# Three of the four weight sums of a seven-product matrix multiplication made by VectorE instead of by accumulating transfers, with X parked in memory

## The reference, cut to what matters

```
h = rmsnorm(x, g[2])
f = square(relu(h @ mlp_w1)) @ mlp_w2     # 2048 -> 8192 -> 2048
x = x + rmsnorm(f, g[3])
```

## Time and profile before

| what | value |
|---|---|
| median of 3 runs | 2440.25 us |
| profiled execution | 2433.57 us, span 2431.7 us |
| mean granted TensorE clock | 0.978 |
| busy: TensorE matmul, weight load | 2312.5 us, 1898.8 us |
| busy: VectorE, ScalarE, GpSimd | 1623.3, 1321.8, 127.4 us |
| read from memory | 559.77 MB |

### The profile page before, as it was taken

The page is one execution under the profiler, slowest core; times in us unless marked ns, Lnnn a source line. Parts: engine busy times, 40 slices in busy tenths (PEclk is TensorE's granted clock), DMA queues, the critical chain, the costliest instruction groups (busy, mean ns, idle before and its releaser), DMA issues.

```text
span 2431.7 us, 26613 instructions
## 1 busy us (share of the span) xinstructions
PE 2312.5 (95%) x10609; PEld 1898.8 (78%) x10609; DVE 1623.3 (67%) x2015; ACT 1321.8 (54%) x1769; POOL 127.4 (5%) x160
## 2 busy tenths in 40 slices
PE   9999999999889899899999989899899899999998
PEld 6778888778778677777887777787777788888887
DVE  5665856866667667667877667667666676556764
ACT  6355445655646556555666646556556555444453
POOL 0000000001001001010001000000000001000000
PEclk9999999999999999999999999999999999999999
DMA  8444545889899898896658898998998845653343
GB/s 332 157 173 173 184 164 190 239 279 275 277 278 254 262 294 254 257 283 228 225 208 233 272 289 252 262 293 264 254 283 269 251 141 201 244 214 129 140 172 121
DMA packets 80299, 563.60 MB, mean 232 GB/s; under 512 B 9033, under 2 KB 9364, under 8 KB 14319
## 3 DMA queue, kind: packets, MB, share of 16 engines
q1 hardware_dynamic: 61568, 429.58, 47.1%
q0 software_dynamic: 18464, 132.20, 26.2%
q10 hardware_dynamic: 144, 0.12, 0.0%
HBM read 559.77 MB, written 2.10 MB: 231 GB/s over the span
## 4 chain that ended last, share of the span: by engine, by line
PE 59%; DMA 23%; DVE 9%; ACT 4%; issue 2%; POOL 1%; ACTq 0%; POOLq 0%; DVEq 0%
PE P L351 56%; DMA R_f<-in_w_u 15%; DVE low L614 7%; DMA raw<-in_w_d 5%; ACT hi L495 3%; DMA raw<-in_w_u 3%; PE P L354 3%; DVE EV L599 1%; DVE R_m L599 1%; ACT EV L551 1%; POOL raw L1002 0%; ACT R_h L490 0%; POOL R_f L1007 0%; DVE R_f_r L599 0%; DVE X L602 0%
## 5 line engine op out<-in xcount | busy, mean ns | idle before, releaser
L614 DVE TENSOR_TENSOR low<-raw,hi 128x1024 fp32r<-128x1024 f32 (+3 forms) x752 | 879.6, 1203 | 535.8 <-ACT hi L495 532.7
L495 ACT ACTIVATE hi<-raw 128x1024 fp32r<-128x1024 f32 (+3 forms) x752 | 758.3, 1039 | 551.2 <-PE P L351 315.4
L351 PE MATMUL P<-hi,R_h 128*128 128x512 f32 (+2 forms) x2944 | 954.9, 395 | 8.4 <-DVE low L614 8.1
L351 PE MATMUL P<-hi,R_f_r 128*128 128x512 f32 x2480 | 822.4, 405 | 96.7 <-DVE R_m L599 52.7
L351 PEld LDWEIGHTS P<-hi,R_h 128*128 128x128 f32 x2944 | 554.4, 189 | 131.4 <-DVE low L614 12.7
L351 PEld LDWEIGHTS P<-hi,R_f_r 128*128 128x128 f32 x2480 | 483.7, 195 | 211.9 <-DVE low L614 109.1
L351 PE MATMUL P<-low,R_h 128*128 128x512 f32 (+2 forms) x1472 | 572.4, 389 | 0.0
L351 PE MATMUL P<-low,R_f_r 128*128 128x512 f32 x1240 | 497.6, 401 | 0.0
L614 DVE TENSOR_TENSOR low<-R_f,hi 128x1024 fp32r<-128x1024 f32 x224 | 264.5, 1221 | 94.1 <-ACT hi L495 92.4
L351 PEld LDWEIGHTS P<-low,R_h 128*128 128x128 f32 x1472 | 278.0, 189 | 56.3 <-issue 4.3
L495 ACT ACTIVATE hi<-R_f 128x1024 fp32r<-128x1024 f32 x224 | 227.7, 1052 | 100.6 <-DMA R_f<-in_w_u 66.4
(11 more groups left out here) (216 smaller groups left out, 1260.4 us busy)
## 6 DMA issues: line engine op xcount, KB each, us to landing
raw<-in_w_d SPq DMA_DIRECT2D x128, 1024.0 KB, 8.4
raw<-in_w_u SPq DMA_DIRECT2D x100, 1024.0 KB, 5.2
R_f<-in_w_u POOLq DMA_DIRECT2D x84, 1024.0 KB, 11.9
raw<-in_w_z SPq DMA_DIRECT2D x46, 1024.0 KB, 4.9
raw<-in_w_i SPq DMA_DIRECT2D x36, 1024.0 KB, 4.8
R_f<-in_w_u SPq DMA_DIRECT2D x28, 1024.0 KB, 7.9
raw<-in_w_u POOLq DMA_DIRECT2D x28, 1024.0 KB, 10.4
raw<-in_w_mo SPq DMA_DIRECT2D x16, 1024.0 KB, 4.9
```

The source lines that it names most:

```text
L351: return self.e.matmul(o, l, r, start=start, stop=stop, skip_group_check=True)
L495: self.e.activation(hi, raw, ACT.Copy).then_inc(*self.inc("high_made", ("high", k, d)))
L614: self.e.tensor_tensor(low, raw, hi.bitcast(f32), ALU.subtract).then_inc(*self.inc("low_made", *lows))
```

## The change

T1, T2 and T3 are made by VectorE. A new `tile_sum` adds two tiles that lie on chip, one 128x2048 instruction each, six in a round. b12 needs two more buffers: these are the two rows of X (`chain[2]`, `chain[3]`), so GpSimd writes X to a memory tensor `x_kept` before the rounds and reads it back after them. b22 is loaded once a round into the ring for product 3, and is kept there until T2 and T3 have been made from it. T4 alone is still an accumulating transfer. Product 2 adds on to product 1 in the same bank (a copy of product 1 is taken first), and product 3 on to product 5; with this two additions of VectorE a round go. Besides: the fourth tile of the kernel lands in `R_f` at once instead of waiting for the ring; and where an MLP or layer begins, two pieces of work of the stage before are issued ahead of two quarter splits.

```diff
+FIRST = 3
-        self.chain = [R_f[:, 4096:6144], R_f[:, 6144:8192]]
+        self.chain = [R_f[:, 4096:6144], R_f[:, 6144:8192], self.X[:, 0, :], self.X[:, 1, :]]
+        self.first_raw = R_f[:, 0:2048]
+    def tile_sum(self, o, i, ready, done):
+        self.wait_ge(ready)
+        self.tt(o, o, i, ALU.add, done)
...
     def link(mlp_, e, s, j, free):
+        w = a[f"w_u{mlp_}"]
+        if s in (0, 1):
+            return
+        if s == 2:
+            E.chain_add(j, m.chain[j], w[8 * e + CHAIN[s + 1] + j], free, ("chained", mlp_, e, s + 1, j))
+        elif e == 7:
+            chain_last[j + 2 * (s == 4)] = free
+        elif s == 3:
+            E.chain_load(j, m.chain[j], w[8 * e + 8 + j], free, ("chained", mlp_, e + 1, 0, j))
         else:
+            E.chain_load(j + 2, m.chain[j + 2], w[8 * e + 12 + j], free, ("linked", mlp_, e + 1, j))
...
             quarter = quarters()
+            out_of(0)
+            squares_of(0)
             quarter(0)
             quarter(1)
-            out_of(0)
-            squares_of(0)
...
+        def keep_x():
+            kept = side_load("kept", a["x_kept"], m.X.rearrange("p t n -> p (t n)"), list(x_m))
+            for j in range(2):
+                E.chain_load(j + 2, m.chain[j + 2], a[up_w][12 + j], [kept, list(h_m), list(r_m)], ("linked", l, 1, j))
...
                 for k in range(4):
-                    x = ready[4 * n + k] if isinstance(ready, list) else ready
+                    x = [ready[4 * n + k] if isinstance(ready, list) else ready, onto]
...
             def third(b, done):
-                k = ev(hold=True)
-                ks[12] = k
-                ms[12] = combine(k, P[b][:, :], EV[ks[5]][:, :], ALU.add, [done, ms[5]], ev_free[k])
-                bank_free[b] = [ms[12]]
+                box["w"] = b, done
             def sixth(b, done):
                 ms[1] = combine(ks[1], P[b][:, :], EV[ks[1]][:, :], ALU.add, [done, ms[1]])
                 bank_free[b] = [ms[1]]
-                c12 = combine(ks[12], EV[ks[12]][:, :], EV[ks[1]][:, :], ALU.subtract, [ms[12], ms[1]])
-                ms[12] = relu_square(ks[12], EV[ks[12]][:, :], 0, c12, None)[1]
-                ms[1] = c12
+                wb, w_done = box["w"]
+                ks[12] = k = ev(hold=True)
+                c12 = combine(k, P[wb][:, :], EV[ks[1]][:, :], ALU.subtract, [w_done, ms[1]], ev_free[k])
+                bank_free[wb] = [c12]
+                ms[12] = relu_square(k, EV[k][:, :], 0, c12, None)[1]
...
+            def first_sum(j):
+                E.tile_sum(m.chain[j], m.chain[j + 2], [("chained", l, e, 0, j), ("linked", l, e, j)], ("chained", l, e, 1, j))
+            def second_sum(j):
+                k = kept_at + j
+                landed = None if listing else plan[k][6]
+                E.tile_sum(m.chain[j], m.raw[(landed or 0) % NL][:, :], [("chained", l, e, 1, j), ("loaded", k)], ("chained", l, e, 2, j))
+            def third_sum(j):
...
+                E.tile_sum(m.chain[j + 2], m.raw[(landed or 0) % NL][:, :], [("linked", l, e, j), ("loaded", k)], done)
...
-            down(0)
-            up(2, 1, HH[:, HRIGHT, TOP], HL[:, HRIGHT, TOP], h_right, plain(b21), second)
+            down(0, lambda: first_sum(0))
+            up(2, 0, HH[:, HRIGHT, TOP], HL[:, HRIGHT, TOP], h_right, plain(b21), second, onto=ms[1], aside=(lambda: first_sum(1), nop))
...
-            up(5, 0, SH[1], SL[1], s_m[1], linked(1), fifth)
-            down(2)
-            up(3, 1, SH[4], SL[4], s_m[4], plain(b22), third)
+            up(5, 1, SH[1], SL[1], s_m[1], linked(1), fifth)
+            down(2, lambda: third_sum(0))
+            up(3, 1, SH[4], SL[4], s_m[4], plain(b22, "kept"), third, onto=ms[5], aside=(lambda: second_sum(0), lambda: second_sum(1)))
             down(3)
-            up(6, 0, SH[2], SL[2], s_m[2], linked(2), sixth)
+            up(6, 0, SH[2], SL[2], s_m[2], linked(2), sixth, aside=(lambda: third_sum(1), nop))
             down(4)
-            up(7, 1, SH[3], SL[3], s_m[3], added, seventh)
+            up(7, 1, SH[3], SL[3], s_m[3], linked(4), seventh)
...
+        back = [side_load(f"back{t}", m.X[:, t, :], a["x_kept"][:, 2048 * t:2048 * t + 2048], chain_last[2 + t]) for t in range(2)]
```

More of the change, by code:

```diff
@@ L997, in side_load @@
         self.e.dma_start(o, i).then_inc(*self.landed(sem, done))
-    def add_tile(self, k, o, i, l):
-        self.wait_ge(("loaded", k))
-        self.e.dma_start(o, i, accum_op=ALU.add).then_inc(*self.landed(f"sum{l % NL}", ("tile sum", k)))
     def chain_add(self, j, o, i, free, done):
@@ L1010, with load_tile @@
 class Sync(Engine):
-    def load_tile(self, k, o, i, l, free):
+    def load_tile(self, k, o, i, ring, free):
         self.wait_ge(free)
-        self.e.dma_start(o, i).then_inc(*self.landed(f"ring{l % NL}", ("loaded", k)))
+        self.e.dma_start(o, i).then_inc(*self.landed(ring, ("loaded", k)))
     def chain_load(self, j, o, i, free, done):
@@ L1070, in load_ahead @@
                     return
[L1071 to L1074, removed]
+                E.load_tile(k, m.raw[l % NL][0:parts, 0:c], a[name][i], f"ring{l % NL}", freed.get(l - NL))
+            elif k == FIRST:
+                E.load_tile(k, m.first_raw, a[name][i], "ring3", None)
             at_["load"] += 1
@@ L1081, in split_part @@
         if kind == "chain":
-            raw, ready = m.chain[more[3]], ("chained", *more)
+            raw, ready = m.chain[more[3] + 2 * (more[2] == 4)], ("chained", *more)
+        elif k == FIRST:
+            raw, ready = m.first_raw, ("loaded", k)
         else:
-            raw, ready = m.raw[l % NL], ("tile sum", k) if kind == "sum" else ("loaded", k, 2 * d // n) if k < 2 else ("loaded", k)
+            raw, ready = m.raw[l % NL], ("loaded", k, 2 * d // n) if k < 2 else ("loaded", k)
         free = None
@@ L1092, in split_part @@
                 link(*more, ("low", k, 3))
-            else:
+            elif kind == "load" and l is not None:
                 freed[l] = ("low", k, 3)
@@ L1097, in link @@
     def link(mlp_, e, s, j, free):
[L1098 to L1103, removed]
-        else:
-            E.chain_add(j, m.chain[j], a[f"w_u{mlp_}"][i], free, done)
-    chain_last = [None, None]
+        w = a[f"w_u{mlp_}"]
[7 more added lines that the diff above has]
+            E.chain_load(j, m.chain[j], w[8 * e + 8 + j], free, ("chained", mlp_, e + 1, 0, j))
+        else:
+            E.chain_load(j + 2, m.chain[j + 2], w[8 * e + 12 + j], free, ("linked", mlp_, e + 1, j))
+    chain_last = [None] * 4
     def split_ahead(n):
@@ L1137, in take @@
             l = o = None
-            if kind != "chain":
+            if kind != "chain" and j != FIRST:
                 l = numbers["landing"]
@@ L1899, in both_ways, with copied @@
         def both_ways(e, up_banks, down_banks):
[L1900 to L1903, removed]
+            b21, b22 = ([8 * e + n + j for j in range(2)] for n in (2, 6))
+            plain = lambda b, kind="load": [(i, kind) for i in b]
+            linked = lambda s: [(8 * e + j, "chain", (l, e, s, j)) for j in range(2)]
             ks, ms, box = {}, {}, {}
+            def copied(n, b, done):
+                k, name = ev(hold=True), mark("product copied")
+                E.copy_out(EV[k][:, :], P[b][:, :], done, ev_free[k], name)
+                ks[n], ms[n] = k, name
             def first(b, done):
[L1907 to L1910, removed]
+                copied(1, b, done)
             def second(b, done):
-                k = ev(hold=True)
[L1914 to L1918, removed]
+                ks[11] = k = ev(hold=True)
+                evacuated, ms[11] = relu_square(k, P[b][:, :], 0, done, ev_free[k])
+                bank_free[b] = [evacuated]
             def fifth(b, done):
[L1921 to L1924, removed]
+                copied(5, b, done)
             def third(b, done):
-                k = ev(hold=True)
-                ks[12] = k
-                ms[12] = combine(k, P[b][:, :], EV[ks[5]][:, :], ALU.add, [done, ms[5]], ev_free[k])
-                bank_free[b] = [ms[12]]
+                box["w"] = b, done
             def sixth(b, done):
@@ L1949, in fourth, with up @@
                 ms[1] = relu_square(ks[1], EV[ks[1]][:, :], 1, c21, None)[1]
+            kept_at = at_["take"] + 9
+            def first_sum(j):
[4 more added lines that the diff above has]
+                E.tile_sum(m.chain[j], m.raw[(landed or 0) % NL][:, :], [("chained", l, e, 1, j), ("loaded", k)], ("chained", l, e, 2, j))
+                if not listing and j == 0:
+                    freed[landed] = ("chained", l, e, 2, j)
+                    load_ahead()
+            def third_sum(j):
+                k = kept_at + j
+                landed = None if listing else plan[k][6]
+                done = ("chained", l, e, 4, j)
+                E.tile_sum(m.chain[j + 2], m.raw[(landed or 0) % NL][:, :], [("linked", l, e, j), ("loaded", k)], done)
+                if not listing and j == 1:
```

(10 more changed lines are left out.)

12 lines of the change are left out of this document (7 added, 5 removed).

## The result

The changed kernel takes 2363.07 us (median of 4 runs, 2362.51 to 2364.74) against 2438.41 (median of 4, 2434.93 to 2447.19) beside it: 0.9687 of the time, 95% interval 0.966 to 0.9714, 75 us less. The forecast was 2396 us, with a range of 2340 to 2436. Its profiled execution took 2364.74 us, 1.7 above its median, where that of before lay under its own.

A forecast was written before the change was run, and what follows sets the result against it. MLP rounds were taken to wait for accumulating transfers. Full rounds -46, openings +6, start -3 and stage beginnings -1 made -44 us against the profiled 2433.57, so 2390; with 6.7 to the median, 2396 us, range 2340 to 2436.

The forecast's parts named there:

- What bounds the kernel: MLP rounds wait for accumulating transfers, one of 25.64 us; a full round loses 10.3 us against 83.6.
- Rival B: Full rounds: no difference, T4's transfer takes 25.6 us, not 11.9; round at 94, kernel 2440 us; chance 0.09.
- VectorE in a full round: VectorE's order makes TensorE wait 0.3 us at d4 and 3.7 at product 7, 4.0 in all, bounds 0 and 8.
- Rival A: Full rounds: everything hidden, no wait reaches the slow clock, rounds of 84 to 85 us, kernel 2322 us; chance 0.22.
- rival C: Full rounds: slower, VectorE sets the pace and all six sums hold up splits; round 99.3, kernel 2512 us; chance 0.09.
- The clock: Behind the wait at product 7, the slow clock costs 2.5 us a full round, between 0 and 3.4.
- PSUM banks: Holding banks instead of rotating: no price at products 1 and 2 or 5 and 3; at product 7 the 3.7 us wait.
- Opening rounds: Two opening rounds: first two sums cost 3.9 us in full; +3 us each, +6 together, bounds 0 and +12.
- X to memory and back: Write of X before the rounds and reading back after: 0; 4 us each if SyncE were needed.
- The start: Kernel's start: the fourth tile lands earlier, -3 us (0 to -4).
- The stage beginnings: Where a stage begins, two places: quarter splits leave the path, -1 us in all (0 to -2.6).
- From the profile to the median: Step from profiled execution to median of runs: the median lies 6.7 us above, taking 2390 to 2396.

The follow-up runs named there:

- e5: Kernel before the change, its eight accumulating transfers a round cut to an eighth of their width, the rest of the sums left out: 2290.8 us, ratio 0.9384.
- e8: Kernel before the change with only the change's use of the banks, all sums by accumulating transfers: 2436.19 us, ratio 0.9974.
- e10: On top of e2, ScalarE's relu and square behind products 6, 7 and 4 issued one d tile later: 2317.32 us, ratio 0.9494.
- e12: On top of e10 with product 3 copied out at once, the last two quarters of X loaded at the kernel's start: 2311.14 us, ratio 0.9477.
- e1: Changed kernel, but ScalarE copies product 3 out of bank 1 at once and c12 is made from the copy: 2338.45 us, ratio 0.9552.
- a1: The changed kernel itself, unaltered, run again beside other experiments: 2364.84 us, ratio 0.9697 to the kernel before.
- e4: Changed kernel with VectorE's six sums a round cut to half their width, the other half left out: 2293.81 us, ratio 0.9396.
- e7: Changed kernel with its side edits undone (fourth tile waits for the ring, quarter splits first again): 2370.2 us, ratio 0.972.
- e2: Changed kernel with the two additions behind product 6 put ahead of the split of T3's second tile on VectorE: 2337.18 us, ratio 0.9547.
- e3: Changed kernel with the edits of e1 and e2 together: 2341.27 us, ratio 0.9563.
- e6: Changed kernel with 12 further 128x512 matmuls ahead of product 7, written to a bank nobody reads: 2343.37 us, ratio 0.9571.

## Why the prediction was right, and where it was off

**What bounds the kernel.** Right: the MLP rounds wait for accumulating transfers (e5). Wrong in the name of the place: I called the product behind the late transfer product 6, and the tile d4. Product 6's pair of additions had run at 1533.35 already; the pair at 1548.20 is product 7's, the tile that waits is d6, and the transfer of 25.64 us is T4's. The first of product 6's two additions, and GpSimd's issues in time with what stood beside T4's transfer, in the kernel before:
```profile
1533.35 0.68 DVE L599 TENSOR_TENSOR EV<-P,EV 128x512 f32<-128x512 f32 x1
...
1514.49 0.86 POOL L1002 DMA_DIRECT2D raw<-in_w_u  x1 [17.23 <-DMA raw<-in_w_u]
1518.10 0.86 POOL L1002 DMA_DIRECT2D raw<-in_w_u  x1 [2.74 <-DMA raw<-in_w_u]
1518.63 2.11 POOL L1007 DMA_DIRECT2D R_f<-in_w_u  x2
```
T4's two additions stood behind T3's two. GpSimd's order cost them little: T2's splits, which they wait for, ended at 1515.1 and 1517.9, and they were issued at 1518.6 and 1519.2. Then four additions were under way at once and landed about 7 us apart, at 1523.2, 1530.0, 1537.4 and 1544.8. e8 has the same, 26.6 us. Rival B lived from that number; with T3's additions gone T4's land in 8.0 us, and B is out.

**VectorE in a full round.** Right in mechanism, place and nearly size: forecast 0.3 us at d4 and 3.7 at product 7, measured 0.4 and 3.0 of standing (0.6 and 3.1 by the gaps between matmuls); no other wait. The dense round: 83.6, measured 83.42 (e5). Rival A stopped at the order, as forecast, and with the order mended (e10 to e12) its rounds of 84 to 85 us are there; rival C would have needed waits elsewhere, and there were none.
**The clock** was the term sized too high: 2.5 us a round for 1.7 (3.4 us at the 1.2 GHz level in each of the twelve). A round came out at 88.87 for 90.1. The old one is 94.41 over the twelve rounds, not the 93.96 that eleven gave: the gain was 5.5 us a round, 66 us, for 46.
**PSUM banks** (the Trainium skill, Perfetto Trace Analysis, Matmuls, on rotating banks): no price at product 2 and 3, as said. At product 7 a half of the answer: TensorE did wait at the bank, yet with the bank free (e1) 2.9 us of the 3.3 stayed. What the bank cost was one long wait in place of short ones, which is to say the clock.
**Opening rounds**: +6 forecast, -0.8 measured, and +0.8 in the second trace of the changed kernel (a1). The failed step is the 3.9 us for the two first sums: d2, the first tile behind VectorE's long stretch, starts 29.2 us into the round before and 31.3 to 31.5 after, so they cost 2.2. They went in part into time in which VectorE had stood for ScalarE, in the kernel before:
```profile
482.81 1.22 DVE L599 TENSOR_TENSOR R_h<-R_m,R_h 128x1024 fp32r<-128x1024 f32 x1 [2.40 <-ACT R_h L490]
```
The wait at product 7, 3.3 us by the gaps, came as forecast, the clock behind it not always. Busy time by stretch behind it, first and second opening round of the changed kernel:
```profile
519.20:522.60 3.40, 3.40 (x15) 2.84 (x16) 1.13 (x1) 3.37 (x5) 0.00 (x0) 1.00 1.00 424
1309.60:1316.20 6.60, 5.75 (x14) 4.52 (x15) 4.19 (x4) 4.45 (x6) 0.00 (x0) 0.50 1.00 423
```
No slow clock in one, twice the usual in the other: this is most of what parts their 91.5 and 94.2 us. In a1 the first had 3.4 us of it and took 93.0. With the sums halved (e4) both take 85.6.
**X to memory and back**: 0 forecast; the part of the trace that holds the write is 0.1 us shorter. Right.
**The start**: wrong. -3 forecast, +0.8 measured here, and -1.0 on the mean of thirteen traces (e7 above). The wait for the fourth tile went, 1.9 us; a longer one came behind it, for a split that stands on ScalarE behind the squares of X's last rows, whose load was queued behind three weight tiles. TensorE's waits near 36 us in the changed kernel, and ScalarE in time:
```profile
PE P L353 <- DVE low L616: 3.4, 1, 3.4
```
```profile
33.84 0.63 ACT L523 ACTIVATE EV<-X 128x512 f32<-128x512 f32 x1 [5.70 <-DMA X<-in_x]
...
36.40 1.99 ACT L497 ACTIVATE hi<-raw 128x1024 fp32r<-128x1024 f32 x2
```
e12 shows it: rows earlier, 4.7 us less. The same start differs by 0.9 us in two executions of the changed kernel (320.2 and 321.1), so a microsecond there is not to be told apart in one pair.
**The stage beginnings**: -1 forecast, -2.4 measured; at the last one (3.4 us of wait before, 1.75 after) the slow clock went as well, though in e2's trace it stood behind a wait of the same length.
**From the profile to the median**: I added 6.7 us, the old execution's place below its median. The new one lay 1.7 above. With the 44 us forecast of the profile against 68.8, this is the rest of the 33 us by which the forecast was too high. The parts did not cancel each other: full rounds 20 us, openings 7, stage beginnings 1 and this step 8 all went one way, the start 4 the other.

## What to carry to other kernels

Lay a tight stretch out in the order of its busiest engine, tile by tile, and it gives the place and size of the wait that will come, where busy shares (75 of 84 us) give neither. When such an engine is short, look first at what it waits for itself: here work that nobody needed soon stood ahead of a rounding on ScalarE and cost 2 us a round. Then look at what waits for the work that was put back, for it has a limit too (e10). Where waits of TensorE can't be removed, several short ones can be better than a long one: in the full rounds here the slow clock came on top of the long one only.

## What was not expected of the hardware

The slow clock behind a single wait of some 3 us in each of the twelve full rounds (3.4 us at 0.50), and none behind waits of 1.45, 1.27 and 0.71 us in one full round (e1, by the gaps between matmuls), though they add up to as much. But the length of the wait doesn't settle it. In the changed kernel's first opening round none followed a wait of 3.1 us; in e3's first opening round one of 1.8 us was followed by 3.4 us at the 1.2 GHz level, its matmul and busy time by stretch:
```profile
517.92 0.50 PE L353 MATMUL P<-hi,R_h 128*128 128x512 f32 x1 [1.80 <-DVE low L616]
...
518.80:522.20 3.40, 3.40 (x10) 2.62 (x9) 3.40 (x4) 3.40 (x5) 0.00 (x0) 0.51 1.01 424
```
And matmuls whose result nobody reads kept the clock at 1.00 and made the kernel some 20 us faster or more (e6), about four fifths of what mending the order brought in e1 and e2.
